# TensorE's products of constants into an unread bank, in five places of a hybrid mixer and expert kernel: left out

## The reference

```python
def reference(x, ...):
    h = layer_norm(x, ln0_g, ln0_b)
    for l in range(DEPTH):                               # 2
        z = h @ w_in[l]                                  # 2048 x 5648
        ...                                              # four mixers -> y_a, y_b, y_c, y_d
        mix = jnp.concatenate([y_a, y_b, y_c, y_d], axis=-1) @ w_out[l]
        h = layer_norm(DN_ALPHA * h + mix, ln1_g[l], ln1_b[l])
        ffn = hier_moe(h, ...)       # group top-1, expert top-2 of 16: silu(x @ w_gate) * (x @ w_up) @ w_down
        h = layer_norm(DN_ALPHA * h + ffn, ln2_g[l], ln2_b[l])
    return h
```

## Time and profile before

| | |
|---|---|
| median of 3 runs | 1750.78 us |
| the profiled execution | 1747.32 us |
| its span | 1745.5 us |
| mean granted TensorE clock | 0.959 of full speed |
| TensorE matmul busy | 1582.0 us (91%), 14804 passes |
| VectorE busy | 921.3 us (53%) |
| ScalarE busy | 523.2 us (30%) |
| read from HBM | 544.04 MB, mean 313 GB/s |

### The profile page before, as it was taken

How to read it: one execution, slowest core, us unless ns; L and a number is a source line. 1 busy time by engine, 2 the same in 40 slices (tenths; PEclk the granted TensorE clock), 3 DMA queues, 4 the chain that set the end, 5 groups by cost and what they waited for, 6 DMA issues and landing times.

```text
span 1745.5 us, 35343 instructions
## 1 busy us (share of the span) xinstructions
PE 1582.0 (91%) x14804; PEld 1068.3 (61%) x14805; DVE 921.3 (53%) x1455; ACT 523.2 (30%) x602; POOL 48.5 (3%) x33
## 2 busy tenths in 40 slices
PE   8999999997999999867699999999889999986664
PEld 8999999885444444322299999998743444432221
DVE  7657655547455555422466466455475455533134
ACT  4553544323122121110254543543231121211011
POOL 0005000000000000000000040000000000000000
PEclk9999999999999999987899989999999999998888
DMA  8554455597999999999965435555979999999996
GB/s 307 195 181 130 161 173 180 193 364 303 421 421 422 421 420 403 423 422 421 407 211 181 163 127 169 169 176 195 416 296 421 421 422 421 414 420 422 422 421 286
DMA packets 139205, 547.26 MB, mean 314 GB/s; under 512 B 23060, under 2 KB 26360, under 8 KB 88568
## 3 DMA queue, kind: packets, MB, share of 16 engines
q1 hardware_dynamic: 138740, 546.13, 80.1%
q10 hardware_dynamic: 388, 0.04, 0.0%
HBM read 544.04 MB, written 2.10 MB: 313 GB/s over the span
## 4 chain that ended last, share of the span: by engine, by line
PE 71%; SPq 15%; DMA 6%; DVE 4%; issue 2%; DVEq 1%; ACT 1%; ACTq 0%
PE ps L776 24%; PE ps L1001 13%; PE ps L913 10%; SPq L419 9%; PE ps L1019 7%; DMA room<-in_w_down_dram 6%; SPq L423 5%; PE ps L773 5%; PE ps L984 4%; PE ps L965 3%; PE ps L973 1%; DVE room L1071 1%; DVE h L1071 1%; PE ps L852 1%; DVE room L1074 0%
## 5 line engine op out<-in xcount | busy, mean ns | idle before, releaser
L1001 PE MATMUL ps<-room 128*32 128x256 f32 x6016 | 374.7, 407 | 102.8 <-DMA room<-in_w_up_dram 94.7
L1071 DVE TENSOR_TENSOR w_lo<-room,w_hi 128x2048 fp32r<-128x2048 f32 x120 | 275.6, 2306 | 244.0 <-ACT w_hi L501 243.5
L1001 PEld LDWEIGHTS ps<-room 128*32 128x32 f32 x6016 | 201.9, 116 | 290.4 <-DMA room<-in_w_up_dram 115.7
L776 PE MATMUL ps<-hT_hi,w_hi 128*128 128x256 f32 x1152 | 330.4, 287 | 2.2 <-DVE hT_lo L1071 2.2
L776 PE MATMUL ps<-hT_hi,w_lo 128*128 128x256 f32 x1152 | 327.3, 284 | 0.0
L776 PE MATMUL ps<-hT_lo,w_hi 128*128 128x256 f32 x1152 | 327.3, 284 | 0.0
L501 ACT ACTIVATE w_hi<-room 128x2048 fp32r<-128x2048 f32 x120 | 228.3, 1914 | 228.6 <-PE ps L776 103.8
L1071 DVE TENSOR_TENSOR h<-h,ps 128x512 f32<-128x512 f32 x376 | 232.8, 681 | 99.2 <-PE ps L984 98.6
L776 PEld LDWEIGHTS ps<-hT_hi,w_hi 128*128 128x128 f32 x1152 | 222.6, 193 | 5.0 <-DVE hT_lo L1071 2.6
L776 PEld LDWEIGHTS ps<-hT_hi,w_lo 128*128 128x128 f32 x1152 | 222.6, 193 | 0.7 <-issue 0.5
L776 PEld LDWEIGHTS ps<-hT_lo,w_hi 128*128 128x128 f32 x1152 | 222.4, 193 | 0.0
(11 more groups left out here) (236 smaller groups left out, 1424.7 us busy)
## 6 DMA issues: line engine op xcount, KB each, us to landing
room<-in_w_gate_dram SPq DMA_DIRECT2D x128, 1024.0 KB, 19.8
room<-in_w_up_dram SPq DMA_DIRECT2D x128, 1024.0 KB, 22.1
room<-in_w_down_dram SPq DMA_DIRECT2D x128, 1024.0 KB, 16.9
room<-in_w_in_dram SPq DMA_DIRECT2D x88, 1024.0 KB, 4.9
room<-in_w_out_dram SPq DMA_DIRECT2D x32, 1024.0 KB, 5.0
room<-in_ln_g_dram SPq DMA_DIRECT2D x5, 1024.0 KB, 5.5
room<-in_ln_b_dram SPq DMA_DIRECT2D x5, 1024.0 KB, 8.2
h<-in_x_dram SPq DMA_DIRECT2D x4, 512.0 KB, 6.4
```

The lines of the kernel that those rows point to most:

```text
L776: last = eng.matmul(ps[:, b + o // 2, (o % 2) * T:(o % 2) * T + T], w_[:, o * P:o * P + P], x_[:, kk, :], start=opens and o % 2 == 0, stop ...
L1001: last = eng.matmul(ps[r0:r0 + BLK, 0, 0:2 * P], xe[:, x0:x0 + BLK], unit_gu(u)[:, :, k, c * P:c * P + P], start=(i == 0 and k == 0), stop ...
L1071: return eng.tensor_tensor(o, a, b, op)
```

## The change

All five calls of `keep_busy` become `pass`. The waits in front of them stay, that of `after_turn` for `hT_act` among them.

```diff
@@ -745,10 +745,10 @@
             def after_turn(n):
 
                 eng.wait_ge(hT_act, 4 * n + 1)
-                keep_busy(10, 0)
+                pass
 
             eng.wait_ge(consts, 1)
-            keep_busy(28, 0)
+            pass
             turn(0, range(8))
             after_turn(0)
             for l in range(L):
@@ -946,7 +946,7 @@
                 last.then_inc(logits_done.sem, 1)
-                keep_busy(14, 7)
+                pass
 
                 eng.wait_ge(m_ready.sem, m_ready.at(l, 1))
 
@@ -954,7 +954,7 @@
                 eng.matmul(ps[:, 1, 32:48], ones[:], M[:, 2, 1, :], start=False, stop=True).then_inc(ranks_done.sem, 1)
-                keep_busy(12, 7)
+                pass
 
@@ -1060,7 +1060,7 @@
                 if l + 1 < L:
                     eng.wait_ge(last_added.sem, last_added.at(l, 4 * NT))
-                    keep_busy(4, 0)
+                    pass
                     turn(2 * l + 2, range(8))
                     after_turn(2 * l + 2)
```

## The result

The change makes the kernel slower, by little and clear of the noise: 1756.15 us against 1750.70, medians of 13 runs each, ratio 1.0029 with a 95% interval of 1.0021 to 1.0038, so 3.7 to 6.7 us. These runs lie between 1749.0 and 1752.0 before and between 1751.9 and 1758.6 after. The profiled execution took 1752.14 us against 1747.32, 4.8 more.

A forecast was written before the change was run, and what follows sets the result against it. TensorE bounds the projections, transfers the experts' stretch, with the logits-to-half-block chain exposed. Terms 0.7 + 0.3 + 1.5 + 0 + 5.6 = 8.1 us slower: 1755.4 on the profiled execution, 1758.9 or 1759 on the 1750.8 median; range 1753 to 1767.

The forecast's parts named there:

- Places 3 and 4: The routing's 14 and 12 products, each layer: without them gaps over 4 us lower the clock; 2.8 us a layer, 5.6 together.
- the gather, over 3.5 us of activity, may have lifted the clock by then: Routing, behind the gather: the clock may be high again, so the four transposes were taken at only 0.2 us.
- no gap takes up any of it: Routing: the 2.8 us a layer passes on whole, since the next weight issue waits for the half block.
- Place 1: The 28 products at the start: without them the first turn runs slow and delays the first projection product 0.7 us.
- Place 2: The 10 products after the turns, twice: idle time before the projections lowers the clock; 0.3 us first layer, 1.5 second.
- Place 5: The 4 products before the second layer's turn: the slower turn stays hidden behind VectorE's weight quarter; 0 us.
- The transfers' stretch: From the ninth weight unit (422 to 862, 1285 to 1724 us): transfers busy throughout, so it ends a fixed time after starting.
- (a): Rival: low stretches are long or in pairs, each routing about 5 us; sum 15.8, so 1766.6 us; chance 0.15.
- (b): Rival: transposes don't lift the clock, so both projections start low; sum 10.6, so 1761.4 us; chance 0.03.
- (c): Rival: no change, the clock rides through the routing's gaps or its loss is hidden; 1752.3 us; chance 0.09.
- (d): Rival: faster, the products of constants stand in the real work's way; 3.5 to 4 us gained, 1747; chance 0.05.

The follow-up runs named there:

- e_route: Kernel before without the 14 and 12 products of constants in the routing, both layers; ratio 1.0033 to the kernel before, 1756.38 against 1750.37 us.
- e_start: Kernel before without the 28 products of constants at the start; ratio 0.9988 to the kernel before, 1748.56 against 1750.37 us.
- e_only_route: Kernel before with only the routing's 14 and 12 products of constants kept, all others left out; ratio 1.0012, 1752.53 against 1749.87 us.
- e_turn: Kernel before without the 10 products of constants behind turns 0 and 2; ratio 0.9997 (0.9988 to 1.0006) to the kernel before.
- e_last: Kernel before without the 4 products of constants ahead of the second layer's turn; ratio 0.9999 (0.9990 to 1.0008) to the kernel before.
- e_transpose_route: Kernel before with 28 and 24 transposes of the same constant in place of the routing's products; ratio 0.9999 (0.9990 to 1.0008).
- e_logits: Kernel before without only the 14 products of constants behind the logits; ratio 1.0001 (0.9990 to 1.0011) to the kernel before.
- e_gap_fill: Kernel before with 10 more products of constants in the gap inside turns 1 and 3; ratio 0.9994 (0.9985 to 1.0003).
- e_ranks: Kernel before without only the 12 products of constants behind the ranks; ratio 1.0020 (1.0009 to 1.0032) to the kernel before.

## Why the prediction was right

The forecast was 1759 us, the median is 1756.15; the sum was 8.1 us, the medians differ by 5.4 and the profiled executions by 4.8. Sign, place and mechanism hold; the sum is too high by about 3 us. The routing was forecast at 5.6 us and took 6.6 in the stages, 1 us more; the other places were forecast at 2.5 us, of which the time of the changed kernel shows nothing beyond e_route's. That the errors are of opposite sign is luck and helped the number.

- **Places 3 and 4, the routing.** Forecast 2.8 us a layer, measured 3.2 and 3.4. The terms, from the order of time of after and before: ranks to gather 6.13 us against 5.31, +0.8 (0.4 forecast); the gather to the transposes 4.35 against 2.63, +1.7 (1.7); from the transposes to the first expert product 4.45 against 3.90 in the first layer and 4.46 against 3.61 in the second, +0.55 and +0.85, and the half block +0.1 and 0 (0.7 forecast for all three). The step "the gather, over 3.5 us of activity, may have lifted the clock by then" failed: the clock stayed low for 17.1 us, up to the first expert products. It cost little, against another step that failed, "no gap takes up any of it": the transposes and the spread took 0.45 and 1.67 us more, and the idle time of 1.46 us (1.17 in the second layer) that stood before the first expert product took up most of that.
- **Place 1.** Forecast 0.7, measured 0.4 in this profile: the 32 transposes took 5.26 us, which at 0.215 and 0.121 each is some 15 slow ones and a slow rate that ended near 17.1 (an estimate), before the pair that VectorE waits for, so the pair came at 17.93 and not at 18.3. In e_start and e_only_route it was 1.1 and 1.0. What failed is a premise that the prediction left unsaid, that the first turn is always fast in the kernel before: in four of the eleven profiles with the 28 products it is not.
- **Place 2.** Mis-sized as a forecast of one execution. The price is right (1.5 us for a stretch of 3.4 us at the start of a projection, e_turn), its occurrence is not: none in the profiled execution of after, two in those of e_turn and e_only_route. 1.8 us were forecast, 0 measured in after, and no loss in e_turn's time.
- **Place 5.** Forecast 0, measured +0.05 (e_last 0.00).
- **The transfers' stretch.** "Ends a fixed time after it starts" holds within 1.5 us in each layer: 438.7 to 439.5 us in the first, but for one stretch of 441.3, and 437.2 to 438.7 in the second, in all kernels. It is shorter by 0.3 and 0.8 us in after, but as short in the second layers of e_turn and e_start, whose routing is that of before. So nothing shows that it gives back what the change took.
- **What the sum lacked** is the stretch in the mixers, +1.4 and -1.4 us in these two executions by their own luck. It adds nothing to their difference and does not explain the 3 us between 8.1 and 5.4. It makes one profile a poor measure of 5 us. It may also account for the 3.5 us that the profiled execution of before lay under its median: that execution has 13.7 us of it in both layers together, others up to 20.5 us, which makes up to 3 us, but the executions without a profile show no stretches.

The rivals: (a), the long low stretches, is half right, 17.1 us long in the routing, but its price of 5 us a layer is refuted by 3.2 and 3.4. (b) falls with e_transpose_route. (c) falls with the clock rows of after. (d), products in the way, shows only in e_logits, where 12 of them follow a low stretch; the 28 of the start end by 12.9 us in every profile here that has them, ahead of the turn.

## What to carry to other kernels

An idle engine's clock is part of the critical path: where a chain of small steps on other engines leaves TensorE idle for some us (4.2 and 4.3 here) just before products that the next transfer waits for, fill the gap with full-width products or transposes, and check in the order of time that they end before the real work is ready. Elsewhere fillers brought no clear gain here: in a gap of 2.4 us whose transposes other engines hid (e_gap_fill), behind the turns and ahead of the second one. Look for low clock where the engine is busy, too: it fell here in a run of many small products, and putting a block of large products in their middle gained 7.7 us (4.5 to 9.4), no less than all five groups of constants together are worth (5.4 us, 3.7 to 6.7). Where low stretches come by chance, compare stage by stage between the same events, since one execution's total carries several us of luck.

## What the runs showed of the hardware that was not expected

- The clock fell while the profile shows TensorE busy without a gap (before, 151.8 to 159.0): in a stretch of 7.2 us of products of 128 columns and of 64 by 64, for 3.4 to 10.2 us, at 1.4 to 1.5 us lost for each 3.4 us.
- In the routing, 28 and 24 passes with full weight loads and 2 columns each left the clock low (gather 3.64 us); 28 and 24 transposes in their place had it high at the gather (1.92 us).
- A gather of 16 passes of 128x512, 3.64 us without a pause, on quarters of 32 columns of the array, did not bring the clock back in either layer of after; in e_ranks the clock was back when the gather ended.
- The profile's record shows 1.00 from 4 to 8 us in before, where 19 passes ran, and from 8 to 12 us, where 38 of the same passes did. The durations decide, not the record.
